# A fifth expert slot, scatter halves around the transposes, streamed shared weights and an earlier router exponential in a hybrid mixture-of-experts trunk

## The chip, the cores and the metric

The kernel runs on one core of a Trainium2 chip. The metric is the device time of one execution in microseconds (us). TensorE (PE) multiplies, VectorE (DVE), ScalarE (ACT) and GpSimd (POOL) do the elementwise work, SyncE (SP) issues the weight transfers, and 16 DMA engines carry them. 1 MiB is 1.049 MB.

## The reference, cut to what matters

Two layers, 256 tokens, width 1024, everything in float32. Each layer is a mixer (layer 0: two sparse-attention groups; layer 1: forgetting attention), a mixture of 64 experts of width 256 with 8 chosen per token plus a shared expert, and a gated per-layer embedding.

```python
for i in range(DEPTH):
    h = even_mixer(...) if i % 2 == 0 else odd_mixer(...)
    x = layer_norm(ALPHA * x + h, ln1_g[i], ln1_b[i])
    m = moe_ffn(x, ...)
    x = layer_norm(ALPHA * x + m, ln2_g[i], ln2_b[i])
    e_i = rms_norm(p[i] @ ple_w_proj[i], ple_norm_g[i])
    x = x + jax.nn.sigmoid(x @ ple_w_gate[i]) * e_i
...
def moe_ffn(x, router_w, router_bias, w1, w3, w2, sw1, sw3, sw2):
    shared = (jax.nn.silu(xf @ sw1) * (xf @ sw3)) @ sw2
    s = jax.nn.sigmoid(xf @ router_w)
    ...                       # 4 of 8 groups, then 8 experts; gates normalised, times 2.5
    # for each expert e, on the tokens that chose it:
    #   y = (silu(xe @ w1[e]) * (xe @ w3[e])) @ w2[e], times its gate, added to its tokens
```

## The kernel before, in words

**Weights.** One expert is w1, w3 and w2 of 1 MiB each (the text calls them gate, lin and down weights), 192 MiB in a layer. All weights of the kernel pass through `ring`, four slots of 3 MiB, in the order of a list `items`: projection pieces, two pieces of the output projection, 64 experts, the embedding's projection and its two gate pieces. SP walks the list and waits before each load for the work that used the slot. In the experts, SP works by pairs (`pair_load`): when PE has done the gate product of pair m (semaphore `exp_gate`), it issues the two gate weights of pair m+2; after the lin product (`exp_up`) the two lin weights; after the down product (`exp_down`) the two down weights. Beside the ring there is spare room (`extra_w1`, `extra_w3`, `extra_w2`, in tiles that are free by then) that takes all of expert 4 and part of expert 10 (`extra_load`, `AGAIN`), and the constants `EARLY` and `NEXT_EARLY` name experts 8 and 14, of which parts go early into the room so won. Expert 4's loads (`extra_load`, L450) are issued when the router's products, the split of x and `y_begin` are done. Experts 0 and 1 are loaded during the attention, 2 and 3 after the output projection.

**The start of a layer's experts.** PE does the output projection, transposes x, and interleaves the router's product with the shared expert's two up products (`shared_up`, L1177: weight columns stationary, 128 tokens moving, 64 products of 128x128 by 128). ACT rounds x to `x_hi` (`x_high`, 2.1 us a tile), copies the transpose, takes the router's exponential and sets `y_acc` to ALPHA * x (`y_begin`); POOL subtracts to get `x_lo`; DVE chooses the experts (`choose`), numbers each expert's tokens (`place`) and builds one-hot matrices.

**The expert loop.** Experts go in 32 pairs; eight experts are an octet of four pairs, u = 0 to 3. Each expert has 64 token slots. `gather` (L1208) fetches an octet's tokens by a product with the one-hot `sel`, a quarter of it in each pair, into one of two sets of buffers (`xe_even`, `xe_odd`). For a pair PE does the gate and the lin product (`exp_up`, L1269, each two experts side by side), the transposes of h (`h_transpose`, L1279), those of the next pair's selection (`sel_transpose`), the down product (`exp_down`, L1309), and the scatter of the pair before (`scatter`, L1331), in two column halves that DVE adds to `y_acc` (`add_y`, L2186). ACT applies SiLU (L1669), which waits for both up products, then copies hT (L1675), and copies y to `y_hi` (L1694); DVE multiplies by the lin half and the slot gate (`gate_h`, L2175), and makes `y_lo` (L2191). One scatter half stands between the gate and the lin product, the other after the transposes, except in the first three and last four pairs, where both stand ahead of the transposes. The shared expert's down products (`shared_down`, L1169) stand in pairs 24 to 27, one each.

**The end.** The last pair's lin and down weights come in column halves. After it: the last scatter, the second norm, the embedding's projection (L1441, waits for its weights) and gate (L1462).

Of the kernel before, what the change touches and what calls it, by code (L numbers as in the profile page):

```python
# [13 lines left out]
P = 128  # L14
# [44 lines left out]
UNROLL = 4  # L59
EARLY = 2 * RING  # L60
AGAIN = EARLY + 2
NEXT_EARLY = AGAIN + RING

# [57 lines left out]
def build_trunk(nc, a, out):  # L121
    with ExitStack() as ctx:
# [5 lines left out]
        def sem(name):  # L128
            if name not in sems:
# [71 lines left out]
        xe_even = (xT[:, :, :].rearrange("p a n -> p (a n)").rearrange("p (c n) -> p c n", c=DC // 2),  # L201
                   proj_flat[:, NT * D:2 * NT * D].rearrange("p (c n) -> p c n", c=DC // 2))
        xe_odd = (pT[:, :, :].rearrange("p a n -> p (a n)").rearrange("p (c n) -> p c n", c=DC // 2),
                  gb_row[:, :, :].rearrange("p a n -> p (a n)").rearrange("p (c n) -> p c n", c=DC // 2))

        def xe(odd, c):

            return (xe_odd if odd else xe_even)[c // 4][:, c % 4, :]

        def xe_two(odd, c):  # L210
            return (xe_odd if odd else xe_even)[c // 4][:, c % 4:c % 4 + 2, :]
# [9 lines left out]
                    (h_silu_all, router_w[:, :, :].rearrange("p c n -> p (c n)")))  # L221
        h_silu = roped[:, 0, 1536:1792]
# [9 lines left out]
        ple_pT = pT[:, 0, 0:512].rearrange("p (c n) -> p c n", c=2)  # L232
# [77 lines left out]
        loaded, w1_loaded_at, down_loaded_at = [], [], []  # L310
        total, w1_total, down_total = [0] * RING, [0] * RING, [0] * RING
        for k, (parts, (_, _, e)) in enumerate(items):
            ffn = parts == "expert"

            signals = not (parts == "expert" and e >= UNROLL and e % 2)
            early = ffn and e == EARLY + 1
            total[k % RING] += 16 * ((1 if ffn else len(parts)) if signals or early or e == NE - 1 else 0)
            down_total[k % RING] += 32 if parts == "expert" and e >= NE - 2 else 16 if ffn and (signals or e == NEXT_EARLY + 1) else 0
            w1_total[k % RING] += 16 if ffn and (signals or early or e == NEXT_EARLY + 1) else 0
            loaded.append(total[k % RING])  # L320
            w1_loaded_at.append(w1_total[k % RING])
            down_loaded_at.append(down_total[k % RING])
# [95 lines left out]
        def _(sp):  # L418
# [1916 lines left out]
```

## Time and profile before

| | |
|---|---|
| median of 3 runs | 1345.64 us (1344.99 to 1346.11) |
| the profiled execution's own time | 1344.79 us |
| its span | 1342.9 us, TensorE clock 1.00 of full speed |
| busy: PE, PE weight loads, DVE, ACT, POOL | 97%, 56%, 35%, 23%, 6% |
| moved by DMA | 462.0 MB, mean 344 GB/s |

The span runs from the first to the last instruction of the profiled execution. Matmuls are pipelined and their ends are modelled, so a busy PE says that PE had work, not that nothing held it back; what it waited for stands in the timeline in brackets, and which stretches were bound by weights shows in the step from pair to pair. Windows give the DMA engines' busy share and their GB/s; those are the rows to read beside PE.

### The profile page before, as it was taken

What the parts mean: (1) busy time and instruction counts of PE and PEld (TensorE: products, weight loads), DVE (VectorE), ACT (ScalarE), POOL (GpSimd) and SP (SyncE); (2) the same over time, 40 slices, a digit from 0 to 9 for tenths busy, and PEclk for the clock granted to TensorE, in tenths of its full rate; (3) what the DMA queues carried; (4) which work ended last, traced back from release to release, by engine and by line L of the source; (5) the groups of instructions that cost most, each with busy time, mean ns of one, the idle gap of its engine ahead of it and who ended that gap; (6) DMA issues with size and microseconds to landing.
All of it is one profiled execution on the core that took longest, in us unless ns stands there. A gap on an engine that the chain in (4) does not pass through costs nothing.

```text
span 1342.9 us, 23014 instructions
## 1 busy us (share of the span) xinstructions
PE 1301.0 (97%) x9694; PEld 746.3 (56%) x9694; DVE 475.1 (35%) x791; ACT 310.3 (23%) x747; POOL 81.2 (6%) x93
## 2 busy tenths in 40 slices
PE   9999999999999999998999999999999999999988
PEld 4555665555555455554488457555555555555544
DVE  1584533333332323333511246232333323233244
ACT  1244422121221221111210234222122221112112
POOL 2443100000000000000100021000000000000000
PEclk9999999999999999999999999999999999999999
DMA  9820689999999999999764537899999999999991
GB/s 306 308 96 32 251 304 415 420 420 421 421 421 420 421 420 420 421 421 394 246 234 145 197 112 277 323 410 421 419 420 421 421 420 421 421 421 421 420 383 76
DMA packets 83151, 462.00 MB, mean 344 GB/s; under 512 B 7024, under 2 KB 7504, under 8 KB 34672
## 3 DMA queue, kind: packets, MB, share of 16 engines
q1 hardware_dynamic: 81040, 454.15, 83.7%
q0 software_dynamic: 2016, 6.43, 1.6%
q8 instruction: 79, 1.29, 0.4%
q14 instruction: 16, 0.13, 0.0%
HBM read 459.50 MB, written 1.05 MB: 343 GB/s over the span
## 4 chain that ended last, share of the span: by engine, by line
PE 78%; DMA 18%; DVE 2%; issue 1%; ACT 0%; SPq 0%; DVEq 0%
PE ps L1269 27%; DMA ring<-in_exp_w_dram 17%; PE ps L1309 12%; PE ps L1331 4%; PE ps L918 4%; PE ps L1462 4%; PE ps L1208 4%; PE ps L1105 3%; PE ps L1023 3%; PE ps L1177 2%; PE ps L1129 2%; PE ps L1279 1%; PE ps L1169 1%; PE ps L1080 1%; PE ps L1441 1%
## 5 line engine op out<-in xcount | busy, mean ns | idle before, releaser
L1309 PE MATMUL ps<-ring,qkT 128*32 128x512 f32 x1984 | 232.9, 595 | 4.1 <-issue 2.8
L2186 DVE TENSOR_TENSOR o_tok<-ps,o_tok 128x1024 f32<-128x1024 f32 x124 | 150.6, 1222 | 156.4 <-PE ps L1331 156.4
L2191 DVE TENSOR_TENSOR y_lo<-ps,y_hi 128x1024 fp32r<-128x1024 f32 x62 | 75.9, 1224 | 213.6 <-ACT y_hi L1694 213.6
L1269 PE MATMUL ps<-ring,xT 128*64 128x256 f32 x1008 | 124.5, 385 | 14.7 <-DMA ring<-in_exp_w_dram 14.6
L1309 PEld LDWEIGHTS ps<-ring,qkT 128*32 128x32 f32 x1984 | 61.5, 109 | 128.8 <-issue 127.6
L1269 PE MATMUL ps<-ring,pT 128*64 128x256 f32 x992 | 124.3, 385 | 5.9 <-DMA ring<-in_exp_w_dram 5.8
L1669 ACT ACTIVATE roped<-ps 128x256 f32<-128x256 f32 x64 | 24.6, 384 | 454.6 <-PE ps L1269 454.6
L1269 PE MATMUL ps<-ring,proj 128*64 128x256 f32 x1008 | 121.8, 379 | 0.0
L1269 PE MATMUL ps<-ring,gb_row 128*64 128x256 f32 x992 | 121.5, 379 | 0.0
L2175 DVE SCALAR_TENSOR_TENSOR roped<-roped,rows,ps 128x256 f32<-128x256 f32 x64 | 30.7, 480 | 236.6 <-ACT roped L1669 236.6
L1269 PEld LDWEIGHTS ps<-ring,xT 128*64 128x64 f32 x1008 | 71.0, 136 | 73.6 <-issue 35.8
L1269 PEld LDWEIGHTS ps<-ring,pT 128*64 128x64 f32 x992 | 69.2, 136 | 67.7 <-issue 36.2
L1694 ACT ACTIVATE y_hi<-ps 128x1024 fp32r<-128x1024 f32 x62 | 63.4, 1023 | 182.9 <-PE ps L1309 182.9
L1269 PEld LDWEIGHTS ps<-ring,proj 128*64 128x64 f32 x1008 | 76.7, 137 | 32.6
L1269 PEld LDWEIGHTS ps<-ring,gb_row 128*64 128x64 f32 x992 | 74.6, 137 | 33.4
L1208 PE MATMUL ps<-sel,x_hi 128*128 128x256 f32 x256 | 69.6, 306 | 0.0
L1208 PE MATMUL ps<-sel,x_lo 128*128 128x256 f32 x256 | 63.3, 281 | 0.0
L1208 PEld LDWEIGHTS ps<-sel,x_hi 128*128 128x128 f32 x256 | 48.3, 189 | 22.4 <-issue 22.4
L1331 PE MATMUL ps<-y_hi,selT 64*128 64x512 f32 x248 | 60.7, 486 | 0.0
L648 POOL DMA_DIRECT2D gb_row<-in_ple_norm_g_dram x2 | 1.5, 737 | 952.0 <-DVEq L1959 952.0
L918 PE MATMUL ps<-ring,xT 128*128 128x512 f32 x128 | 57.8, 600 | 0.0
L1462 PE MATMUL ps<-ring,xT 128*128 128x512 f32 (+1 forms) x144 | 55.9, 546 | 0.7 <-ACT xT L1473 0.7
(308 smaller groups left out, 1464.3 us busy)
## 6 DMA issues: line engine op xcount, KB each, us to landing
ring<-in_exp_w_dram SPq DMA_DIRECT2D x158, 2048.0 KB, 22.8
ring<-in_exp_w_dram SPq DMA_DIRECT2D x54, 1024.0 KB, 8.8
ring<-in_od_w_in_dram SPq DMA_DIRECT2D x6, 2048.0 KB, 8.6
ring<-in_ple_w_gate_dram SPq DMA_DIRECT2D x4, 2048.0 KB, 15.4
ring<-in_ev_w_in_dram SPq DMA_DIRECT2D x3, 2048.0 KB, 20.0
ring<-in_ev_w_o_dram SPq DMA_DIRECT2D x2, 2048.0 KB, 10.4
x_tok<-in_exp_w_dram SPq DMA_DIRECT2D x4, 1024.0 KB, 7.6
ring<-in_exp_w_dram SPq DMA_DIRECT2D x8, 512.0 KB, 17.9
```

Of the source, the lines that this page charges most:

```text
L918: ins = pe.matmul(ps[:, 2 * t + n, :], xT[:, c, t * P:(t + 1) * P], w[:, c, :], start=(c == 0), stop=(c == DC - 1))
L1023: ins = pe.matmul(ps[:, proj_bank(j, t), 0:c1 - c0], xT[:, c, t * P:(t + 1) * P], w[:, c, :], start=(c == 0), stop=(c == DC - 1))
L1105: ins = pe.matmul(ps[:, (2 * j + half) % 4, b * SEQ:(b + 1) * SEQ], w[:, c, (2 * half + b) * P:(2 * half + b + 1) * P], xT[:, c, :], start ...
L1208: ins = pe.matmul(by_tile[:, :, t, :], part[:, t, (2 * j + c) * P:(2 * j + c + 1) * P], sel[:, t, :].rearrange("p (e s) -> p e s", e=8), s ...
L1269: ins = pe.matmul(ps[b * SLOTS:(b + 1) * SLOTS, 2, w * FE:(w + 1) * FE], xe(odd, c)[:, u * P + b * SLOTS:u * P + (b + 1) * SLOTS], views[b ...
L1309: ins = pe.matmul(ps[q:q + TILE_SLOTS, 4 + half, :], hT[:, f, h0:h0 + TILE_SLOTS], down_rows(b, f, half), start=(f == 0), stop=(f == 1))
L1331: ins = pe.matmul(ps[:, bank + t, :], selT[tile_rows(t), par, :], part[tile_rows(t), half * PIECE:(half + 1) * PIECE], start=(part is y_hi ...
L1462: ins = pe.matmul(ps[:, part_bank(t, n, i), cols], xT[:, c, t * P:(t + 1) * P], w[:, c, cols], start=(c == 0), stop=(c == DC - 1), skip_gr ...
L1694: act.activation(y_hi[:, :], ps[:, 4:6, :], ACT.Copy).then_inc(sem("y_high"), 1)
L2175: dve.scalar_tensor_tensor(h_exp, h_silu, slot_gate[:, par:par + 1], ps[:, 2, FE:2 * FE], ALU.mult, ALU.mult)\
L2186: dve.tensor_tensor(ys, ps[:, bank:bank + 2, :], ys, ALU.add).then_inc(sem("y_added"), 1)
L2191: dve.tensor_tensor(y_lo[:, :], ps[:, 4:6, :].rearrange("p b n -> p (b n)"), y_hi[:, :], ALU.subtract)\
```

## The change

- The ring's four slots, the spare room (`FIFTH`) and, for expert 1 alone, one more room (`APART`: `o_tok`, half of `qkT`, `gb_row`) become homes of experts: 0 to 4 by `EARLY_HOMES`, all others by `CYCLE`, five homes in turn. Slot 0, which held expert 1, now takes expert 5 at that place. Everything is loaded in single experts of three loads of 1 MiB; the fifth home's down weights are three loads, row f = 0 in pieces of 4 KB, row f = 1 in two column halves with pieces of 2 KB.
- `pair_load(L, m)` frees by rooms: after pair 0 only expert 6 is loaded, after pair 1 experts 7 and 8, then 2m+5 and 2m+6; after pair 28 experts 61 and 62, after pair 29 expert 63 and the halves.
- Expert 1's gate weights are requested ahead of the shared expert's, expert 4's lin and half of its down weights behind those; the rest of experts 1 and 4 after the split of x (`fifth_load`). `y_begin` moves from ACT to POOL, after the first gate product.
- `shared_up` has the tokens stationary and the weights moving (32 products of 128x128 by 256); the shared h is transposed in pair 24 (`shared_turn`), and its down products go to pairs 25, 26, 28 and 29. The transposes of p move inside pair 28.
- `router_exp` stands ahead of `x_high`; the placing product waits for `chosen` and not for the gates.
- In the loop, gate and lin products stand back to back (banks 2 and 3), SiLU waits for the gate product alone, one scatter half stands ahead of the transposes and one behind; the whole gather of the next octet is in u = 3, with one set of buffers.

```diff
-UNROLL = 4
-EARLY = 2 * RING
-AGAIN = EARLY + 2
-NEXT_EARLY = AGAIN + RING
+FIFTH = RING
+APART = RING + 1
+EARLY_HOMES = (3, APART, 1, 2, FIFTH)
+CYCLE = (0, 3, 1, 2, FIFTH)
+SHARED_TURN = PAIRS - 8
+SHARED_AT = (PAIRS - 7, PAIRS - 6, PAIRS - 4, PAIRS - 3)
+
+
+def home(e):
+
+    return EARLY_HOMES[e] if e < len(EARLY_HOMES) else CYCLE[e % len(CYCLE)]
+
+
+def room_of(e):
+
+    return {6: 0, 7: 2, 8: 3}.get(e, e - len(CYCLE))
...
+            def pair_load(L, m):
+
+                after = [e for e in range(6, NE) if room_of(e) // 2 == m]
+                whole = [e for e in after if e < NE - 2]
+                sp.wait_ge(sem("exp_gate"), L * PAIRS + m + 1)
+                for e in after:
+                    gate_load(L, e)
+                sp.wait_ge(sem("exp_up"), L * PAIRS + m + 1)
+                for e in whole:
+                    lin_load(L, e)
+                if NE - 1 in after:
+                    last_lin_load(L)
+                sp.wait_ge(sem("exp_down"), L * PAIRS + m + 1)
+                for e in whole:
+                    down_load(L, e)
+                if NE - 1 in after:
+                    last_down_load(L)
...
+            def apart_gate_load(L):
+
+                if L == 0:
+                    sp.wait_ge(sem("qkT_tp"), len(QKT_BATCHES) + NT)
+                else:
+                    sp.wait_ge(sem(f"ple_out{L - 1}"), 2 * NT)
+                gate_load(L, 1)
+
+            def fifth_load(L):
 
                 sp.wait_ge(sem("router_mm"), NT * (L + 1))
                 sp.wait_ge(sem("x_split"), NT * (L + 1))
-                sp.wait_ge(sem("y_begun"), NT * (L + 1))
-                sp.dma_start(extra_w1, a["exp_w1"][L, RING].rearrange("(p c) f -> p c f", c=DC)).then_inc(sem("extra_loaded"), 16)
-                sp.dma_start(extra_w3, a["exp_w3"][L, RING].rearrange("(p c) f -> p c f", c=DC)).then_inc(sem("extra_loaded"), 16)
-                extra_down_load(L, RING)
-
-            def extra_down_load(L, e):
-
-                rows_f = a["exp_w2"][L, e].rearrange("(p f) n -> p f n", f=2)
-                for f in range(2):
-                    if f:
-                        sp.wait_ge(sem("shared_h"), NT * (L + 1))
-                    for half in range(2):
-                        sp.dma_start(extra_w2[f][half], rows_f[:, f, half * PIECE:(half + 1) * PIECE]).then_inc(sem("extra_loaded"), 16)
+                gate_load(L, 4)
+                sp.wait_ge(sem("shared_w1_used"), L + 1)
+                lin_load(L, 1)
+                sp.wait_ge(sem("gb_used"), NT * (3 * L + 1))
+                down_load(L, 1)
+                sp.wait_ge(sem("shared_h"), NT * (L + 1))
+                down_load(L, 4, (1,))
...
                     if k == e0 + 2:
+                        apart_gate_load(L)
                         shared_load(L)
+                        lin_load(L, 4)
+                        down_load(L, 4, (0,))
...
+                pool.wait_ge(sem("exp_gate"), L * PAIRS + 1)
+                for t in range(NT):
+                    step(pool.tensor_tensor(y_acc[:, t, :].rearrange("p (n c) -> p n c", c=DC),
+                                            x_hi[:, t, :].rearrange("p (c n) -> p n c", c=DC),
+                                            x_lo[:, t, :].rearrange("p (c n) -> p n c", c=DC), ALU.add))
+                    pool.tensor_scalar(y_acc[:, t, :], y_acc[:, t, :], ALPHA, None, ALU.mult).then_inc(sem("y_begun"), 1)
...
-                def shared_up(t, blocks):
-
-                    for n in blocks:
-                        for c in range(DC):
-                            ins = pe.matmul(ps[:, 4 + t, n * P:(n + 1) * P], (shared_w1, shared_w3)[n // 2][:, c, n % 2::2],
-                                            xT[:, c, t * P:(t + 1) * P], start=(c == 0), stop=(c == DC - 1))
+                def shared_up(t, w, c0, c1):
+
+                    for c in range(c0, c1):
+                        ins = pe.matmul(ps[:, 4 + t, w * FE:(w + 1) * FE], xT[:, c, t * P:(t + 1) * P],
+                                        (shared_w1, shared_w3)[w][:, c, :], start=(c == 0), stop=(c == DC - 1))
                     return ins
 
+                def shared_turn():
+
+                    pe.wait_ge(sem("shared_h"), NT * (L + 1))
+                    pe.wait_ge(sem("y_added"), 2 * (L * PAIRS + SHARED_TURN - 1))
+                    for f in range(2):
+                        for t in range(NT):
+                            ins = pe.transpose(ps[:, 1, f * SEQ + t * P:f * SEQ + (t + 1) * P],
+                                               h_all[:, t * FE + f:(t + 1) * FE:2], ident)
+                    ins.then_inc(sem("shared_tp"), 1)
...
+                def pe_step(m, o, u, gather_next=True, selT_next=True, scatter_last=True):
 
                     par = u % 2
-                    inside = scatter_last and gather_next and not (o == 0 and u < 3)
-                    late = o == 0 and u == 3
-                    exp_up(m, o, odd, u, par, first and M0 == 0, scatter_half=inside, gather_inside=late)
-                    if scatter_last and not inside:
-                        if o == 0:
-                            pe.wait_ge(sem("xe_copied"), 4 * O0 + 5)
+                    gathers = gather_next and u == 3
+                    if m + M0 > 0:
+                        pe.wait_ge(sem("exp_h"), m + M0)
+                    if m > 0:
+                        pe.wait_ge(sem("selT_copied"), m + (M0 + 1))
+                    exp_up(m, o, u, 0)
+                    if gathers:
                         scatter(m - 1, 0, 1 - par)
-                        scatter(m - 1, 1, 1 - par, bank=0)
-                    own_gather = gather_next and (o > 0 or u == 0)
-                    if own_gather or late:
-                        j = 2 if late else u
-                        pe.wait_ge(sem("xe_copied"), 4 * o + (4 * O0 + 4 + j))
-                        if m >= PAIRS - 8:
-                            pe.wait_ge(sem("shared_added"), 4 * L + m - (PAIRS - 8) + 1)
-                        gather(o + 1, j, halves=(0, 1) if scatter_last else (0,))
+                    if m == PAIRS - 4:
+                        pe.wait_ge(sem("xe_copied"), 4 * OCTETS + 4 * O0)
+                        pe.wait_ge(sem("y_added"), 2 * (M0 + m - 1))
+                        for t in range(NT):
+                            for c in range(2):
+                                ins = pe.transpose(ps[:, 0, c * SEQ + t * P:c * SEQ + (t + 1) * P], p_tok[:, t, c::2], ident)
+                            ins.then_inc(sem(f"pT_tp{L}"), 1)
+                    if m == SHARED_TURN:
+                        shared_turn()
+                    if m in SHARED_AT:
+                        shared_down(SHARED_AT.index(m))
+                    if gathers:
+                        gather(o + 1, 0)
+                    exp_up(m, o, u, 1)
+                    if gathers:
+                        scatter(m - 1, 1, 1 - par)
+                    elif scatter_last:
+                        scatter(m - 1, 0, 1 - par)
                     h_transpose(m)
                     if selT_next:
                         sel_transpose(m + 1, o + 1 if u == 3 else o, (u + 1) % 4)
-                    if own_gather and not scatter_last:
-                        gather(o + 1, u, halves=(1,))
-                    if inside:
-                        scatter(m - 1, 1, 1 - par)
-                    exp_down(m, par, first and M0 == 0, by_half=not selT_next)
-                    if late:
-                        pe.wait_ge(sem("xe_copied"), 4 * O0 + 7)
-                        gather(1, 3)
-
+                    if scatter_last and not gathers:
+                        if m == SHARED_TURN:
+                            pe.wait_ge(sem("shared_hT"), L + 1)
+                        if m in SHARED_AT:
+                            pe.wait_ge(sem("shared_added"), 4 * L + SHARED_AT.index(m) + 1)
+                        scatter(m - 1, 1, 1 - par, bank=0)
+                    if gathers:
+                        pe.wait_ge(sem("xe_copied"), 4 * o + (4 * O0 + 5))
+                        gather(o + 1, 1)
+                    exp_down(m, 0, by_half=not selT_next)
+                    if gathers:
+                        pe.wait_ge(sem("xe_copied"), 4 * o + (4 * O0 + 6))
+                        gather(o + 1, 2)
+                    exp_down(m, 1, by_half=not selT_next)
+                    if gathers:
+                        pe.wait_ge(sem("xe_copied"), 4 * o + (4 * O0 + 7))
+                        gather(o + 1, 3)
...
-                def y_begin(t):
-                    act.activation(y_acc[:, t, :], x_tok[:, t, :], ACT.Copy, scale=ALPHA).then_inc(sem("y_begun"), 1)
-
                 rsqrt_guess()
-                x_high(0)
                 copy_T("xT_act", tp, 0)
                 router_exp(0)
-                y_begin(0)
+                x_high(0)
                 rsqrt_guess()
-                x_high(1)
                 copy_T("xT_act", tp, 1)
                 router_exp(1)
-                y_begin(1)
+                x_high(1)
                 shared_silu(0)
                 shared_silu(1)
...
-                    act.wait_ge(sem("exp_up"), m + (M0 + 1))
+                    act.wait_ge(sem("exp_gate"), m + (M0 + 1))
```

## Rows read from the trace of the kernel before

**Rows 1.** The page: GB/s in 40 slices, and the chain's shares.

```profile
GB/s 306 308 96 32 251 304 415 420 420 421 421 421 420 421 420 420 421 421 394 246 234 145 197 112 277 323 410 421 419 420 421 421 420 421 421 421 421 420 383 76
...
PE 78%; DMA 18%; DVE 2%; issue 1%; ACT 0%; SPq 0%; DVEq 0%
```

**Rows 2.** PE's timeline, one pair: start, duration, line; down products at 408.19 and 422.07.

```profile
408.19 3.64 PE L1309 MATMUL ps<-ring,qkT 128*32 128x512 f32 x32
...
419.73 0.38 PE L1208 MATMUL ps<-sel,x_hi 128*128 128x256 f32 x1
...
420.80 0.50 PE L1279 MATMUL ps<-const,roped 128*128 128x128 f32 x2
...
422.07 3.64 PE L1309 MATMUL ps<-ring,qkT 128*32 128x512 f32 x32
```

**Rows 3.** PE's waits between 200 and 700 us: total, times, longest.

```profile
PE ps L1269 <- DMA ring<-in_exp_w_dram: 10.8, 16, 1.7
```

**Rows 4.** PE's timeline, the last two pairs of layer 0.

```profile
612.72 1.95 PE L1269 MATMUL ps<-ring,xT 128*64 128x256 f32 x16 [1.68 <-DMA ring<-in_exp_w_dram]
...
618.47 3.64 PE L1309 MATMUL ps<-ring,qkT 128*32 128x512 f32 x32 [0.34 <-issue]
622.77 1.95 PE L1269 MATMUL ps<-ring,xT 128*64 128x256 f32 x16 [0.66 <-DMA ring<-in_exp_w_dram]
...
631.97 3.64 PE L1309 MATMUL ps<-ring,qkT 128*32 128x512 f32 x32 [0.52 <-issue]
```

**Rows 5.** Windows of layer 0; last two columns: DMA engines' busy share, GB/s.

```profile
180.00:185.00 5.00, 5.00 (x47) 3.25 (x44) 0.00 (x0) 0.28 (x1) 0.00 (x0) 1.00 0.52 184
185.00:190.00 5.00, 4.60 (x42) 2.04 (x45) 0.48 (x1) 1.83 (x6) 0.00 (x0) 1.00 1.00 423
190.00:194.00 4.00, 4.00 (x40) 2.33 (x34) 1.23 (x1) 1.02 (x1) 0.00 (x0) 1.00 0.91 348
...
195.00:200.00 5.00, 4.50 (x45) 2.74 (x45) 1.82 (x3) 1.07 (x5) 0.00 (x0) 1.00 1.00 356
...
280.00:400.00 120.00, 120.00 (x1041) 64.17 (x1038) 39.38 (x45) 27.21 (x63) 0.00 (x0) 1.00 1.01 420
```

**Rows 6.** The same windows view, two stretches with pieces of 2 KB.

```profile
14.00:22.00 8.00, 8.00 (x20) 3.61 (x19) 0.13 (x1) 0.60 (x1) 2.40 (x5) 1.00 1.05 388
...
224.00:228.00 4.00, 4.00 (x37) 2.55 (x37) 0.48 (x1) 1.45 (x3) 0.00 (x0) 1.00 1.02 364
```

**Rows 7.** The chain before the experts of layer 0 (first and last part of four).

```profile
155.43 5.65 PE ps L1177 x48
...
171.67 1.94 PE ps L1177 x16
```

**Rows 8.** One line, L1105 (layer 1's projection): duration min/median/max, first and last start.

```profile
L1105 PE MATMUL ps<-xT,ring x192: 379/379/380, 693.6 to 734.8; 128*128 128x256 f32 x192
```

**Rows 9.** SP's timeline: the first loads after pairs 0 and 1.

```profile
181.26 0.33 SPq L495 DMA_DIRECT2D ring<-in_exp_w_dram  x1
...
194.30 0.38 SPq L530 DMA_DIRECT2D ring<-in_exp_w_dram  x1
```

**Rows 10.** DMA issues: KB each, median us from issue to landing.

```profile
qkT<-in_sh_w_dram SPq DMA_DIRECT2D x2, 1024.0 KB, 4.7
```

**Rows 11.** PE's timeline, pairs 0 and 1 of layer 0.

```profile
184.60 0.39 PE L1208 MATMUL ps<-sel,x_hi 128*128 128x256 f32 x1
...
185.74 0.50 PE L1279 MATMUL ps<-const,roped 128*128 128x128 f32 x2 [0.40 <-DVE roped L2175]
...
199.95 0.64 PE L1309 MATMUL ps<-ring,qkT 128*32 128x512 f32 x4 [0.50 <-ACT qkT L1675]
```

**Rows 12.** The chain of waits at the end of layer 1's experts.

```profile
1301.66 0.78 issue
```

**Rows 13.** ACT's and POOL's timelines: router exponential, then x_lo of tile 1.

```profile
165.60 0.22 ACT L1629 ACTIVATE rows<-ps 128x64 f32<-128x64 f32 x1 [1.01 <-PE ps L883]
...
162.89 2.87 POOL L705 TENSOR_TENSOR x_lo<-x_tok,x_hi 128x1024 fp32r<-128x1024 f32 x1 [13.79 <-ACT x_hi L1624]
```

More of the change, by code:

```diff
@@ L306, in release_value @@
             return sem(f"ple_mm{L}"), NT * 2 + n if n else NT
[L310 to L322, printed above, removed]
-        w_loaded = [sem(f"w_loaded{s}") for s in range(RING)]
-        down_loaded = [sem(f"down_loaded{s}") for s in range(RING)]
-        w1_loaded = [sem(f"w1_loaded{s}") for s in range(RING)]
+        assert all(expert_item[L] % RING == EARLY_HOMES[0] for L in range(DEPTH))
+        loaded, gate_at, lin_at, down_at = {}, {}, {}, {}
+        gate_total, lin_total, down_total = [0] * (APART + 1), [0] * (APART + 1), [0] * (APART + 1)
+        for k, (parts, (_, L, e)) in enumerate(items):
+            if parts != "expert":
+                lin_total[k % RING] += 16 * len(parts)
+                loaded[k] = lin_total[k % RING]
+                continue
+            at = home(e)
+            gate_total[at] += 16
+            lin_total[at] += 16
+            down_total[at] += 48 if at == FIFTH else 32 if e >= NE - 2 else 16
+            gate_at[L, e], lin_at[L, e], down_at[L, e] = gate_total[at], lin_total[at], down_total[at]
+        w_loaded = [sem(f"w_loaded{s}") for s in range(APART + 1)]
+        down_loaded = [sem(f"down_loaded{s}") for s in range(APART + 1)]
+        w1_loaded = [sem(f"w1_loaded{s}") for s in range(APART + 1)]
         def slot_view(k, n, c):
@@ new lines, in ffn_load, with last_lin_load @@
+            def ffn_load(L, e):
+                gate_load(L, e)
+                lin_load(L, e)
+                down_load(L, e)
+            def last_lin_load(L):
+                s, e = home(NE - 2), NE - 2
+                for half in range(2):
+                    cols = slice(half * UP_N // 2, (half + 1) * UP_N // 2)
+                    sp.dma_start(ring[:, s:s + 2, UP_N + cols.start:UP_N + cols.stop],
+                                 a["exp_w3"][L, e:e + 2].rearrange("e (p c) f -> p e (c f)", c=DC)[:, :, cols])\
+                      .then_inc(w_loaded[s + half], 16)
@@ L565, in _ @@
+                    if k == e0 + RING:
+                        fifth_load(L)
+                        for m in range(PAIRS - 2):
+                            pair_load(L, m)
                         k = e0 + NE
@@ L1677, in selT_copy @@
                 def selT_copy(m, par):
-                    bank = 3 if isinstance(m, int) and m == 0 else 2
+                    bank = 6 if isinstance(m, int) and m == 0 else 2
                     act.wait_ge(sem("selT_tp"), m + (M0 + 1))
@@ L2237, in dve_step @@
                         y_low(m)
-                    if build_bf and u == 2:
+                    if gather_next and u == 2:
                         sel_bf_build(o + 1)
```

421 lines of the change are left out of this document (171 added, 250 removed).

## The prediction

> **What bounds the kernel now.** I read the page first, then windows, PE's timeline, PE's waits, SP's timeline and the chain. The page's slices show two long plateaus at 420 GB/s, one for each layer's experts, and idle DMA engines between them [rows 1]. The chain gives PE 78% and DMA 18% [rows 1], which alone would call it a PE kernel. The step from pair to pair says more. Undisturbed, one pair takes PE 13.9 us (408.19 to 422.07) [rows 2]. Its weights, 6 MiB or 6.29 MB at 420 GB/s [rows 5], take 15.0 us, or 2.5 us for 1 MiB. So PE eats up what was loaded ahead and then waits: 16 times in layer 0, 10.8 us in all [rows 3], the last times at 612.72 and 622.77 [rows 4]. From 185 us on the DMA engines never rest (busy share 0.91 to 1.01 [rows 5]). A layer's end is thus set by three things: how many weights are there when the unbroken stream begins, how fast the stream runs, and how much PE work remains after the last arrival that PE waits for. PE's own order inside a pair counts only where PE isn't waiting for weights, so SiLU's earlier start, the scatter halves and the gathers gathered into u = 3 gain nothing in mid-loop as long as they add less than the 10.8 us of waits. A pair without a gather falls by the 1.1 us of one (419.73 to 420.80 [rows 2]), one with u = 3 rises by three times that, and five homes hold 15 MiB, 37 us of stream, which bridges the uneven pairs. I cost all of it at nothing; with that cover gone it would be 0.1 to 0.2 us a pair.
>
> **Part by part, layer 0; layer 1 repeats it.**
>
> (a) *The lead of the stream.* Before, experts 0 to 4 (15 MiB) are in by 180 us, and the next requests go out at 181.26, when pair 0's gate product is done [rows 9]. Afterwards expert 5 takes the place of 1, and 1 and 4 use the idle time, so 18 MiB are in; but pair 0 frees room for expert 6 alone, and 7 and 8 must wait for pair 1's gate product. When is that? The shared products shrink from 128 entries at 5.65/48 = 0.118 us [rows 7], 15.1 us, to 64 entries at 41.2/191 = 0.216 us [rows 8], 13.8 us: the loop starts 1.3 us earlier. Pair 0 loses a gather of 1.1 us that covered waits, and gets the waits instead: gate_h alone, some 0.7 of the 1.14 us between 184.60 and 185.74, and the 0.5 us for hT that pair 1 shows at 199.95 [rows 11]; the balance is 0.3 us less. So the request seen at 194.30 [rows 9] goes out at 192.7, and with a start-up of 4.7 - 2.5 = 2.2 us [rows 10] the stream is unbroken from 194.9 with 21 MiB in. Before, by then: 15 MiB and (184 + 423) x 5 + 348 x 4.9 = 4.7 MB [rows 5], 19.5 MiB, and then 195 to 200 runs at 356 instead of 420 GB/s, 0.3 MiB lost. The lead is 1.8 MiB: **-4.5 us** (-3 if the new stream has the same slow stretch and a later start, -5.5 at most).
>
> (b) *Small pieces.* Eleven experts in the stream (9, 14, ... 59) now bring their down weights half in pieces of 4 KB, half in 2 KB. The long stretch of 2 KB pieces ran at 388 GB/s [rows 6]: half a MiB costs 0.10 us more than at 420, the 4 KB half I put at half that, 0.15 x 11 - 0.2 for expert 10, which had such pieces before: 1.4 us. The stretch that holds expert 10's pieces ran at 364 GB/s for 4 us [rows 6]: what it carried would take 3.5 us at 420, 0.5 us for 1 MiB, so 0.25 + 0.13 in eleven experts, less 0.5: 3.7 us. I take **+2.2 us**, nearer the first, which is the longer sample. The Trainium skill (DMA: Bandwidth & Descriptors, Specifications) puts the smallest transfer at line rate at 512 B; by it these pieces cost nothing and the sum would be 2.2 us a layer lower. Both windows here speak against it.
>
> (c) *The order of the last loads.* Before, the gate weights of pair 31 come 4 MiB behind the lin weights of pair 30: 10.05 us (612.72 to 622.77 [rows 4]) and PE, which needs 10.05 - 0.66 - 0.34 = 9.05 us for the work between, has to wait for them. Afterwards pair 30 is experts 60 and 61 from different requests: lin 61 is followed by down 61, gate 63 and then the last halves. PE waits for lin 61 and then still has 9.05 us of work, while gate 63 lands after 5.0 us. So pair 31 begins 4.05 us behind the stream, where before it began with it: **+4.0 us** (0 if PE were not held at lin 61 at all, 4.5 if pairs 28 and 29, which now carry shared products behind the heavy pair 27, leave it later still).
>
> (d) *The last pair.* A scatter half between transposes and down product covers the 0.52 us wait at 631.97 [rows 4]: **-0.5 us**. The Exp ahead of the rounding, and the placing product without the gates, lie beside shared products that keep PE busy: nothing.
>
> (e) *After layer 1* PE stands 0.78 us before the embedding's projection, whose weights are behind the stream [rows 12]; a lead of 2 us removes it: **-0.7 us**, once. y_begin on POOL: two adds of 2.87 us [rows 13] and two scalings lie between pair 0's gate product and the first add_y some 18 us later: nothing.
>
> Sum: 2 x (-4.5 + 2.2 + 4.0 - 0.5) - 0.7 = +1.7 us, so 1346.5 us against the profiled execution's 1344.79 (span 1342.9 and 1.9 around it). The median of the runs is 0.85 us above that execution: **1347.3 us**, 0.1% more. What a measurement of this kernel tells from no change is about 0.2%, 2.7 us, so this is no change.
>
> **Rivals.** *The tail costs nothing* (c = 0): PE reaches pair 30 late anyway, or lin 61 arrives early because the DMA engines finish unevenly, and the lead reaches the end: 1347.3 - 8.0 = 1339.3. For it: the stretches of waiting are short; against: 1.68 us of waiting at just that place [rows 4]. *Small pieces cost nothing*: the DMA engines move pieces of 2 and 4 KB at the rate of 8 KB, and 1347.3 - 2 x 2.2 = 1342.9 remains; both windows [rows 6] are against it. (This is how the Trainium skill's page named in (b) has it.) *Small pieces are dear*, 3.7 us a layer as in the shorter window: 1347.3 + 2 x 1.5 = 1350.3. *Expert 1 comes late*: its lin weights are asked for only after the split of x, behind expert 4's gate weights. The exponential at 165.60 moves up about a microsecond, then rounding (2.1) and x_lo of 2.87 us [rows 13] end the split at about 170, where it ended at 165.8; plus 2.2 and two MiB, it lands at 177.2. PE wants it 3.55 us into the loop, at 179.8. It decides from 2.6 us of delay, and then every microsecond is paid in both layers, for the stream waits on PE there. With 3 us: 1353.3. For it: SP's queue holds expert 1's down weights, expert 4's rest and all of pair_load behind that one wait.
>
> **How the numbers follow.** Likeliest, the sum as it stands: 0.42, own range 1344 to 1349. Tail free 0.17, pieces free 0.11: together 0.28 faster by over 0.2%. Pieces dear 0.14, expert 1 late 0.16: 0.30 slower. Within 0.2%: 0.42. The range 1338.5 to 1352 leaves out the outer part of the late expert (0.1) and the two gains together (0.05).
>
> **What would show it.** Right: windows at 420 GB/s from about 195 us; steps of some 12.7 and 17 us early in the loop; PE's first waits for weights near pair 14, earlier than pair 18, because it runs faster; a wait before pair 30's lin product and none before pair 31's gate product; L1177 at 13.8 us a layer. Wrong: a wait at pair 31 too (then c is too high), windows clearly below 415 GB/s in the loop (b too low), a wait in pair 0 for weights (the late expert), or waits for ACT or DVE in most pairs, which would make PE's own order the bound.

## The result, and the profile after

The changed kernel is slower by a little: 1350.76 us against 1345.57 us (medians of 6 runs each), a ratio of 1.0038, 95% interval 1.0026 to 1.005, so 5.2 us. A second measurement of both gave 1349.55 against 1344.37 us, 1.0037 (1.0022 to 1.0053). The profiled execution took 1350.55 us, with a span of 1348.4 us, 5.5 us more than before.

The page of the changed kernel: GB/s in 40 slices and the chain's shares.

```profile
GB/s 306 306 95 63 297 272 418 418 419 418 421 418 419 419 420 418 419 419 370 230 220 159 197 126 269 323 420 418 419 419 419 418 420 420 419 418 419 419 355 63
...
PE 77%; DMA 11%; DVE 6%; SPq 4%; issue 1%; ACT 1%; DVEq 0%
```

Beside [rows 1] three things stand out. The plateaus lie for the most part at 418 to 419 GB/s where they lay at 420 to 421. The DMA share of the chain fell from 18% to 11%, but SP's queue (SPq) rose from 0% to 4%: the chain now runs in part through SP's issue of loads, some of which held SP for 2.13 us and more. PE itself waits for weights nearly as long as before, 9.8 us in layer 0 for 10.8. And VectorE (DVE), at 2% before, now has 6% of the chain. That last figure points to the part of the change that I had costed at nothing; the chain has 19.2 us of VectorE between 150 and 185 us, and 5.4 us in the kernel of experiment one.

**Where the time went.** I took three distances in PE's timeline, for each layer, in every kernel: from the first shared product (L1178, before L1177) to the first gate product of the expert loop; from the down product of pair 0 to that of pair 31; and the sum that a layer's stretch makes, first shared product to pair 31's down product.

```
us, layer 0 / layer 1         shared to loop   pair 0 to pair 31   whole stretch
before                        22.29 / 22.29    444.95 / 444.18     476.71 / 475.94
changed                       23.82 / 23.85    445.89 / 445.90     478.67 / 478.80
changed, second profile       23.85 / 23.84    445.49 / 445.76     478.29 / 478.65
```

The stretch grew by 2.0 and 2.9 us. The forecast was +1.2 in each layer. After layer 1 the 0.78 us of [rows 12] are gone (pair 31's down product to the embedding's projection: 5.42 us, before 6.25). In this one execution PE's granted clock also fell to half in layer 1's attention, and the stretch from layer 0's last down product to layer 1's first shared product took 189.86 us for 188.28. So 1.96 + 2.86 - 0.83 + 1.58 = 5.6 us, less 0.1 us at the start of the program: the 5.5 us of the span.

**The prologue.** PE's timeline of the changed kernel from the first shared product to the first gather, layer 0 (start, duration, line; idle before in brackets). Neighbours in this pipelined view overlap, so read the starts.

```profile
155.17 3.62 PE L1178 MATMUL ps<-qkT,xT 128*128 128x256 f32 x16
158.62 2.32 PE L1178 MATMUL ps<-pT,xT 128*128 128x256 f32 x10
161.71 1.16 PE L721 MATMUL ps<-const,x_tok 128*128 128x128 f32 x8 [0.76 <-DVEq L1951]
...
169.24 1.89 PE L1178 MATMUL ps<-pT,xT 128*128 128x256 f32 x8
172.20 0.66 PE L1204 MATMUL ps<-roped,const 128*128 128x64 f32 x4 [1.08 <-DVE roped L1928]
172.70 1.95 PE L1178 MATMUL ps<-pT,xT 128*128 128x256 f32 x8
174.81 0.36 PE L1220 MATMUL ps<-sel,x_hi 128*128 128x256 f32 x1 [0.17 <-DVE sel L2138]
```

The shared products are as cheap as I said: 16 of them from 155.17 to 158.62, 0.216 us each, 13.8 us for 64. But PE stands idle three times, 2.0 us in all, each time for VectorE, and none of these waits was there before. What holds VectorE shows in its own timeline and in GpSimd's (POOL), here in layer 1, tile 0:

```profile
820.57 0.15 DVE L1919 MATCH_REPLACE8 rows<-rows 128x8 f32<-128x8 f32 x1
820.75 2.22 DVE L1921 TENSOR_SCALAR rows<-rows 128x8 f32<-128x8 f32 x1
823.01 0.23 DVE L1924 SCALAR_TENSOR_TENSOR rows<-rows 128x64 f32<-128x64 f32 x1
...
820.09 2.86 POOL L699 TENSOR_TENSOR x_lo<-x_tok,x_hi 128x1024 fp32r<-128x1024 f32 x1 [29.88 <-ACT x_hi L1624]
```

A tensor_scalar of 8 elements a partition takes 2.22 us. It ends at 822.97, and GpSimd's subtraction, under way since 820.09, ends at 822.95. The source view has all four of them, one a tile:

```profile
L1921 DVE TENSOR_SCALAR rows<-rows x4: 2207/2274/2328, 152.2 to 837.3; 128x8 f32<-128x8 f32 x4
```

The same instruction before, L1929, took 171 to 172 ns in all four places. There the rounding on ScalarE came first and x_lo ran while VectorE stood waiting for the router's exponential. In layer 1, tile 1, the kernel before shows (VectorE, then GpSimd):

```profile
830.85 0.20 DVE L1917 TENSOR_SCALAR rows<-rows 128x64 f32<-128x64 f32 x1 [3.18 <-ACT rows L1629]
...
827.86 2.88 POOL L705 TENSOR_TENSOR x_lo<-x_tok,x_hi 128x1024 fp32r<-128x1024 f32 x1 [13.77 <-ACT x_hi L1624]
```

x_lo sat in a gap of 3.18 us and was over 0.1 us before VectorE went on. The change put it behind the exponential and the 2 us of the rounding, and so into the router's chain. (The Trainium skill, "SBUF — State Buffer", Who interferes with whom, has this as an exclusive lock: VectorE and GpSimd share one pair of ports, a tensor_scalar can use it, and whoever comes second is blocked until the other's instruction ends. The rows agree, 822.97 beside 822.95.)

**The tail.** PE's waits for weights from 200 to 700 us, where [rows 3] had 16 of 10.8 us:

```profile
PE ps L1264 <- DMA ring<-in_exp_w_dram: 8.2, 9, 1.3
PE ps L1264 <- DMA x_tok<-in_exp_w_dram: 1.6, 1, 1.6
```

The last of them is at 504.38 us. From there to the end of the layer PE never waits for weights, where it waited at 612.72 and 622.77 before [rows 4]. Layer 1 is the same but for one wait of 0.44 us at 1238.92, and the second profile has two such short ones (0.17 and 0.37 us). Eight steps of PE alone (pair 23's down product at 515.86 to pair 31's at 633.84, 118.0 us) set the end.

**The stream.** Windows of the changed kernel, answering to [rows 5], and SP's first requests, answering to [rows 9]:

```profile
180.00:185.00 5.00, 5.00 (x50) 3.34 (x48) 0.00 (x0) 0.64 (x4) 0.00 (x0) 1.00 0.55 185
185.00:190.00 5.00, 3.85 (x39) 1.69 (x39) 1.15 (x3) 0.70 (x4) 2.85 (x1) 1.00 0.91 339
190.00:195.00 5.00, 5.00 (x48) 2.68 (x42) 1.23 (x1) 1.02 (x1) 4.91 (x3) 1.00 0.51 162
195.00:200.00 5.00, 5.00 (x47) 3.00 (x43) 0.48 (x1) 0.56 (x2) 4.91 (x2) 1.00 0.89 341
280.00:400.00 120.00, 119.64 (x1027) 64.57 (x1024) 37.44 (x42) 29.99 (x64) 0.00 (x0) 1.00 1.02 419
```

```profile
182.71 0.33 SPq L437 DMA_DIRECT2D ring<-in_exp_w_dram  x1
...
195.23 1.05 SPq L437 DMA_DIRECT2D ring<-in_exp_w_dram  x2
```

The requests behind pair 1's gate product go out at 195.23 instead of the 192.7 I forecast. By 200 us the changed kernel has moved 44.1 MB, the kernel before 43.0 MB (windows of 0 to 200 us): a lead of 1.1 MiB, not 1.8. At 419 GB/s against 421 a part of it is lost on the way.

### The profile page after: what moved, and what is told of

Read it like the earlier page. It is cut to its first block, busy times and chain, and to the rows that moved or that the text cites. A ratio compares the mean times of both kernels' runs of the same rounds, so it can differ in the third digit from the quotient of the medians.

```text
span 1348.4 us, 22909 instructions
## 1 busy us (share of the span) xinstructions
PE 1306.5 (97%) x9574; PEld 739.7 (55%) x9574; DVE 485.1 (36%) x793; ACT 317.4 (24%) x743; POOL 108.0 (8%) x101
## 4 chain that ended last, share of the span: by engine, by line
PE 77%; DMA 11%; DVE 6%; SPq 4%; issue 1%; ACT 1%; DVEq 0%
PE ps L1264 26%; PE ps L1294 13%; DMA ring<-in_exp_w_dram 7%; PE ps L1220 5%; PE ps L1317 4%; PE ps L1462 4%; DMA x_tok<-in_exp_w_dram 4%; PE ps L919 3%; PE ps L1106 3%; PE ps L1024 3%; PE ps L1130 2%; PE ps L1274 2%; SPq L462 1%; SPq L437 1%; PE ps L1081 1%
## 5 line engine op out<-in xcount | busy, mean ns | idle before, releaser
L1264 PE MATMUL ps<-ring,xT 128*64 128x256 f32 x1632 | 247.2, 384 | 11.7 <-DMA ring<-in_exp_w_dram 8.8
L1264 PE MATMUL ps<-ring,pT 128*64 128x256 f32 x1632 | 242.7, 379 | 0.0
L1264 PEld LDWEIGHTS ps<-ring,xT 128*64 128x64 f32 x1632 | 138.1, 137 | 101.9 <-issue 51.7
L1264 PEld LDWEIGHTS ps<-ring,pT 128*64 128x64 f32 x1632 | 146.7, 137 | 57.2
L1294 PEld LDWEIGHTS ps<-ring,qkT 128*32 128x32 f32 x1632 | 56.8, 109 | 106.0 <-issue 103.3
L1668 ACT ACTIVATE qkT<-ps 128x256 f32<-128x256 f32 x64 | 24.6, 385 | 240.3 <-PE ps L1274 239.2
L1294 PE MATMUL ps<-roped,qkT 128*32 128x512 f32 x288 | 67.6, 597 | 0.0
L1656 ACT ACTIVATE xT<-ps 128x1024 f32<-128x1024 f32 x32 | 32.7, 1025 | 86.5 <-PE ps L1264 71.4
L1264 PE MATMUL ps<-proj,xT 128*64 128x256 f32 x192 | 45.9, 382 | 4.9 <-DMA ring<-in_exp_w_dram 4.9
## 6 DMA issues: line engine op xcount, KB each, us to landing
ring<-in_ple_w_gate_dram SPq DMA_DIRECT2D x4, 2048.0 KB, 12.6
roped<-in_exp_w_dram SPq DMA_DIRECT2D x24, 256.0 KB, 19.2
```

The costliest lines, as they stand in the source:

```text
L1264: ins = pe.matmul(ps[b * SLOTS:(b + 1) * SLOTS, 2 + w, w * FE:(w + 1) * FE], xe(c)[:, u * P + b * SLOTS:u * P + (b + 1) * SLOTS], views[b] ...
L1294: ins = pe.matmul(ps[q:q + TILE_SLOTS, 4 + half, :], hT[:, f, h0:h0 + TILE_SLOTS], down_rows[b](f, half), start=(f == 0), stop=(f == 1))
L1656: act.activation(xe_two(2 * j), ps[:, bank:bank + 2, :], ACT.Copy).then_inc(sem("xe_copied"), 1)
```

## The experiments

Each ran beside the kernel before on the same chip. Ratios are to it, with the 95% interval; the changed kernel stands at 1.0037 or 1.0038 by the same measure.

**One: the rounding ahead of the exponential again.**

```diff
 rsqrt_guess()
+x_high(0)
 copy_T("xT_act", tp, 0)
 router_exp(0)
-x_high(0)
 rsqrt_guess()
+x_high(1)
 copy_T("xT_act", tp, 1)
 router_exp(1)
-x_high(1)
```

> The changed kernel with ScalarE's rounding of x put back ahead of the router's exponential. Theory H (GpSimd's subtraction x_lo now lies over the router's chain on VectorE and holds its tensor_scalar L1921 for 2.2 us instead of 0.17, once for each tile): L1921 falls to 0.17 us, PE's waits of 0.76 us before the transposes of tile 1 and of 1.08 us before the placing product go, the expert loop starts about 2.8 us earlier in each layer, and 4 to 5.5 us come off in all: 1345 to 1347 us. Rival (VectorE's chain is late because the shared product takes PE less time, whatever the order on ScalarE): L1921 may fall, but the loop starts where it did, 1350 to 1351 us. Rival (the tail decides, PE has no room from 504 us on, and what the prologue gains is waited for at the weights): the loop starts earlier, and the time falls by under 1.5 us.

Measured: 1344.66 us, 0.9998 (0.9989 to 1.0007), by the ratios 0.4% or 5.4 us less than the changed kernel. The source view:

```profile
L1921 DVE TENSOR_SCALAR rows<-rows x4: 171/172/172, 152.8 to 832.8; 128x8 f32<-128x8 f32 x4
```

The waits before the transposes and the placing product are gone, and the shared products reach the loop in 21.41 and 21.43 us, 2.4 us sooner than in the changed kernel and 0.9 sooner than before. Theory H holds, and the rival of the tail falls: the layer ends sooner by the same 2.4 to 2.8 us. The start moved a little less than the 2.8 us that I expected.

**Two: the exponential ahead of the rounding, in the kernel before.** The mirror image of the same lines in the kernel before, with y_begin still behind each.

> The kernel before with the exponential put ahead of the rounding, that part of the change alone. Theory H: the tensor_scalar L1929 takes 2.2 us instead of 0.17 for each tile; about 1 us of the first hold is covered by VectorE's wait for the products (0.98 us), the second is not, so the placing product waits 2 to 3 us and the loop starts 2 to 3 us later a layer: 1348.5 to 1351.5 us. Rival (the exponential comes earlier, the chain is shorter or the same): 1344.5 to 1346 us.

Measured: 1353.73 us, 1.0064 (1.0049 to 1.0078). The hold appears in the kernel that had none:

```profile
L1929 DVE TENSOR_SCALAR rows<-rows x4: 2212/2299/2381, 154.3 to 838.9; 128x8 f32<-128x8 f32 x4
```

PE waits 0.75 us before the transposes and 1.65 us before the placing product, and the loop starts 2.9 us later in layer 0. The sign and the place are as H says; the time is above what I expected. In the profiled execution 2.0 us of the rest lie before the experts of layer 0, and 1.5 us are a fall of PE's clock behind the wait of 1.66 us in layer 1 (granted 0.52 from 844 to 846 us). Why the median of the runs is as high, I haven't settled.

**Three: the shared products earlier.**

```diff
-SHARED_TURN = PAIRS - 8
-SHARED_AT = (PAIRS - 7, PAIRS - 6, PAIRS - 4, PAIRS - 3)
+SHARED_TURN = 16
+SHARED_AT = (17, 18, 20, 21)
```

(VectorE's loop over the octets ends at octet 3, so that pairs 16 to 23 stand with fixed numbers.)

> The changed kernel with the shared expert's transposes in pair 16 and its four down products in pairs 17, 18, 20 and 21, where PE waits for weights, instead of pair 24 and pairs 25, 26, 28 and 29. Theory T (from 504 us on PE never waits for weights again, so the 9.5 us of shared work in the last eight pairs are on the path): waits for weights appear again before the last pairs, and a layer ends 1.5 to 3 us sooner, 1345 to 1348 us. Rival (the stream sets the end and the shared work is hidden in it wherever it stands): 1350 to 1351.5 us. Rival (shared work in pairs 17 to 21 delays the down products and with them the requests): slower than 1351.5 us.

Measured: 1347.46 us, 1.0019 (1.001 to 1.0028), by the ratios 2.5 us less than the changed kernel. The waits are back, 7.8 us of them from 510 us on in layer 0, the last two before pair 30's down product:

```profile
611.41 1.95 PE L1264 MATMUL ps<-ring,xT 128*64 128x256 f32 x16 [0.88 <-DMA ring<-in_exp_w_dram]
616.38 1.95 PE L1264 MATMUL ps<-ring,xT 128*64 128x256 f32 x16 [1.29 <-DMA ring<-in_exp_w_dram]
...
621.96 3.64 PE L1294 MATMUL ps<-ring,qkT 128*32 128x512 f32 x32
634.39 1.92 PE L1294 MATMUL ps<-ring,qkT 128*32 128x512 f32 x16
```

But the stretch is shorter by only 0.4 and 0.8 us (478.25 and 478.02 against 478.67 and 478.80; against the second profile of the changed kernel, 478.29 and 478.65, by 0.04 and 0.6). Experiment six repeats the 0.4 and 0.8 against one. So the shared work did set the end, and the stream stood about a microsecond or less behind it. My 1.5 to 3 us a layer were too high, by the medians (1.2 a layer) too, though the time lies in the range that I gave. Part of the medians' 2.5 us stands in none of the three distances.

**Four: the fifth home's down weights whole.** From expert 9 on they go to gb_row, which expert 1 has left, in pieces of 8 KB.

```diff
-down_total[at] += 48 if at == FIFTH else ...
+down_total[at] += 48 if e == FIFTH else ...
...
-elif to == APART:
+elif to == APART or e > FIFTH:
     sp.dma_start(first_w2[:, :, :], rows_f).then_inc(down_loaded[to], 16)
```

> The changed kernel with the down weights of experts 9, 14, ..., 59 loaded as one piece of 8 KB a partition into gb_row, which expert 1 has left, instead of one piece of 4 KB and two of 2 KB. Theory P (the small pieces slow the stream, term b): the windows of the loop rise from 418 to 419 to 420 to 421 GB/s, PE's last wait for weights in the layer comes about 1.3 us sooner, and so does the layer's end: 1347.5 to 1349.5 us. Rival (small pieces cost nothing, the slower stream has another cause): windows at 418 to 419 and 1350 to 1351.5 us. Rival (they cost what b's upper bound said, 0.34 us an expert): 1344 to 1346 us.

Measured: 1346.35 us, 1.0004 (0.9993 to 1.0016). The window of 280 to 400 us:

```profile
280.00:400.00 120.00, 120.00 (x1032) 64.51 (x1027) 37.43 (x42) 30.22 (x64) 0.00 (x0) 1.00 1.01 421
```

421 for 419 GB/s, and pair 0 to pair 31 takes 444.31 and 444.39 us for 445.89 and 445.90: 1.5 us a layer (1.2 and 1.4 against the second profile, 445.49 and 445.76). That is theory P by the windows and the distances. The time is lower than I expected for it (1347.5 to 1349.5): the median fell by 4.4 us, 3.1 of them in these stretches, the rest in none of the three distances. The DMA engines are busy all through both windows (1.02 and 1.01), so it is the rate of the pieces and no pause of the stream; and SP's queue, 4% of the chain in the changed kernel, is at 0% here.

**Five: x_lo in four instructions of a quarter each**, in the order of the changed kernel.

> The changed kernel with GpSimd's x_lo of each tile made in four instructions of a quarter each (about 0.72 us) instead of one of 2.86 us; order and results as before. Theory H as a lock held for one instruction: L1921 waits for the end of the quarter under way at most, 0.3 to 0.9 us instead of 2.2, the loop starts 1 to 2.4 us earlier a layer, 1345.5 to 1349 us. Rival (VectorE and GpSimd share bandwidth for as long as GpSimd is at work): L1921 stays at 2.2 us, 1350 to 1351.5 us. Rival (GpSimd's queue takes the lock again before VectorE gets it): L1921 at 1.5 to 2.2 us, no gain.

Measured: 1347.1 us, 1.0009 (1.0 to 1.0017). VectorE in layer 1, tile 1, while GpSimd's quarters (0.86 us each) run from 834.13 to 837.43:

```profile
834.69 0.33 DVE L1924 TENSOR_SCALAR rows<-rows 128x8 f32<-128x8 f32 x1
835.05 0.83 DVE L1927 SCALAR_TENSOR_TENSOR rows<-rows 128x64 f32<-128x64 f32 x1
835.92 0.23 DVE L1928 MAX8 rows<-rows 128x8 f32<-128x64 f32 x1
...
836.73 0.78 DVE L1933 TENSOR_TENSOR gates<-rows,roped 128x64 f32<-128x64 f32 x1
```

The tensor_scalar takes 0.22 to 0.33 us instead of 2.2 (L1924 is L1921 with three lines more above it), though GpSimd is at work just as long. So the hold lasts as long as one instruction of the other engine and no more, and shared bandwidth is ruled out. The loop starts after 22.14 us instead of 23.85. Two more instructions are held here: the scalar_tensor_tensor and the tensor_tensor, both with both tensors in SBUF and 0.22 us elsewhere, take 0.83 and 0.78. Each held instruction ends 0.02 to 0.08 us after a GpSimd quarter, as the whole holds of 2.2 us end 0.02 to 0.03 us after the whole subtraction. MAX8 beside the same quarters isn't held (0.23 us, as in the kernel before).

**Six to eight: the edits together.** Six is one and three, seven is one, three and four, and eight is seven with this:

```diff
 for e in after:
-    gate_load(L, e)
+    if e != NE - 2:
+        gate_load(L, e)
 sp.wait_ge(sem("exp_up"), L * PAIRS + m + 1)
 for e in whole:
     lin_load(L, e)
+if NE - 2 in after:
+    gate_load(L, NE - 2)
```

> Both: the rounding ahead of the exponential, and the shared products in pairs 16 to 21. In the two single runs the layer from pair 0's to pair 31's down product took 445.5 and 445.9 us with the first, 445.5 and 445.1 us with the second, against 445.9 in the changed kernel, so the stream stands right behind PE in the tail. If the two add up, the loop starts 2.4 us earlier as in the first and the tail is 0.4 to 0.8 us a layer shorter as in the second: 1342.5 to 1344 us. If the first's lead of the stream comes free only with a light tail, 1340 to 1342 us.

> The same two and the down weights of experts 9, 14, ..., 59 in pieces of 8 KB. Alone, this took 1.5 us a layer off the loop (444.3 and 444.4 instead of 445.9 us). With a tail that is bound by the stream, the whole difference of 418.7 to 421 GB/s over 440 us counts, 2.4 us a layer: 1338 to 1340.5 us. Rival (the shared products of the tail were what the stream hid, and nothing adds up): 1341 to 1344 us.

> The kernel with all three, and expert 62's gate weights asked for behind expert 61's lin weights instead of ahead of them. Step c of the prediction (PE is held at lin 61 and pair 31 then begins behind the stream): lin 61 lands 2.5 us earlier, PE's waits before pair 30's down product, 2.2 us in the run with the early shared products, go or fall below 0.7 us, and 1.5 to 2.2 us a layer come off against the kernel with all three. Rival (the last pair's weights bind as soon as lin 61 does not): the waits move to pair 31 and under 0.7 us a layer is gained.

```
                        median   ratio, 95% interval        shared to loop   whole stretch, layer 0 / 1
one                     1344.66  0.9998 (0.9989 to 1.0007)  21.41            475.86 / 476.37
six (one, three)        1342.71  0.9984 (0.9975 to 0.9993)  21.42            475.51 / 475.60
seven (and four)        1339.42  0.9958 (0.9945 to 0.9971)  21.41            473.85 / 474.09
eight (and gate 62)     1336.14  0.9937 (0.9924 to 0.995)   21.41            473.16 / 472.64
```

The edits add up. Six is 0.4 and 0.8 us a layer below one, as three was below the changed kernel. Seven takes 1.7 and 1.5 us more off, less than the 2.4 that I expected for a tail bound by the stream, and eight 0.7 and 1.5 us in the profiled executions, 3.3 us in the medians; in layer 0 that is less than the 1.5 to 2.2 us that I expected, and its profiled execution had a fall of the clock there (561.8 us). Seven's tail, PE's timeline:

```profile
606.40 1.95 PE L1266 MATMUL ps<-ring,xT 128*64 128x256 f32 x16 [0.73 <-DMA ring<-in_exp_w_dram]
611.37 1.95 PE L1266 MATMUL ps<-ring,xT 128*64 128x256 f32 x16 [1.30 <-DMA ring<-in_exp_w_dram]
616.96 3.64 PE L1296 MATMUL ps<-ring,qkT 128*32 128x512 f32 x32
629.39 3.64 PE L1296 MATMUL ps<-ring,qkT 128*32 128x512 f32 x32
```

PE is held at pair 30's gate and lin products (2.03 us) and at nothing behind them. In eight, layer 0, both waits are gone, and the two down products stand at 615.08 and 627.52; in layer 1 one of 0.73 us is left. Eight is the fastest of all: 0.6% below the kernel before, 1.0% below the changed one.

**Nine and ten: the order of the last loads alone, and the changed kernel again.**

> The changed kernel with nothing but expert 62's gate weights asked for behind expert 61's lin weights. Theory T (in the changed kernel PE has 118 us of work behind its last wait for weights in layer 0, so the order of the last loads cannot show): the down product of pair 31 follows that of pair 23 at the same distance as before the edit, 118 us, and the time is that of the changed kernel within 0.7 us. Rival (the order of the last loads costs its 1.9 us a layer here too, as it did in the kernel with all three edits): 3 to 4 us less.

> The changed kernel, unedited, beside the run before on the same chip. Every theory: 1349.5 to 1351.5 us, L1921 at 2.2 us. Whether the TensorE clock falls to half in layer 1's attention again (it did in the profiled execution at 771 us, for 3.3 us) is open: if it is part of the change, it should be there again; if it is a matter of the single execution, it may stand elsewhere or be missing, and the span is then some 1.6 us shorter.

Measured: 1349.53 us, 1.004 (1.0028 to 1.0053), and 1349.55 us, 1.0037 (1.0022 to 1.0053). The edit that is worth 3.3 us behind the other three is worth nothing alone: pair 23's to pair 31's down product takes 118.33 us with it and 118.23 without. The second profile of the changed kernel shows no fall of the clock (span 1346.5 us), so that fall is no part of the change.

## Why the prediction was right or wrong

The forecast was 1347.3 us, 0.1% more; it came to 1350.76, inside the range, but 0.38% more: one of the "slower" outcomes that had 0.30, not "no change". The sum had a term missing and a mechanism in the wrong place. That it came so near is luck in part, for the two errors have opposite signs. With the missing term taken out (experiment one), the stretches are 0.8 us shorter and 0.4 us longer than before, where the sum has +1.2 in each layer: what it does contain is 2.0 and 0.8 us too high, and what it lacks is 2.8 and 2.4 us. The time lands on the 1350.3 of *small pieces are dear*, but not for that reason.

**The step that failed** is the sentence in (d) that "the Exp ahead of the rounding" lies "beside shared products that keep PE busy: nothing". It costs 2.4 us at the start of each layer's loop, by experiment one, and it is the whole loss: without it the kernel measures the same as before. I had the rows in hand, x_lo of 2.87 us and the exponential [rows 13], and moved x_lo only as far as the split of x was concerned, not against the instructions that it would now lie beside on another engine. Nor had the exponential anything to gain: PE's router products of tile 1 ended at 830.56 us in the kernel before, and the exponential began at 830.59. The rounding ahead of it had never delayed it. Moved ahead, it began at 165.93 us in layer 0, where [rows 13] had 165.60; the prediction had it about a microsecond sooner.

**(a), the lead.** The shared products shrank by the 1.3 us forecast, and the hold ate that and 1.5 us more, so the loop began later instead of earlier, and the lead was 1.1 MiB for 1.8. With the hold removed (experiment one) it is 1.8 MiB at 200 us, as worked out: 193 GB/s over 140 us and 298 over 60, 44.9 MB, against 43.0. The 4.5 us of it reach the end only in part. Eight, with (b), the tail's shared work and the order of the last loads mended, is 3.6 and 3.3 us a layer below the kernel before, where (a) and (d) promised 5.0.

**(b), small pieces.** Right in mechanism; for +2.2 us a layer the distances show 1.2 to 1.7 (experiments four and seven), the medians 2.2 and 1.6. The rival *small pieces cost nothing*, which is how the Trainium skill would have it (DMA: Bandwidth & Descriptors, Specifications), falls by experiments four and seven. So does *small pieces are dear*.

**(c), the last loads.** Right as a mechanism and wrong for this kernel. It assumed that PE is held at lin 61. In the changed kernel PE isn't held at pairs 28 to 31 in either layer, because pair 24 to pair 29 carry the shared work and pair 27 a whole gather; experiment nine shows the order to cost nothing there. My own bracket, "4.5 if pairs 28 and 29 leave it later still", named the ground and not the consequence: if PE is late by itself, the loads' order doesn't enter at all. In its place stands PE's own work, only 0.4 to 0.8 us a layer ahead of the stream (experiment three). Once PE is held at lin 61, in seven, waits stand where (c) put them and none before pair 31, and a single MiB moved back is worth 1.6 us a layer by the medians, 0.7 and 1.5 by the distances; (c)'s full 4.0 was not tested.

**(d) and (e).** The last pair's wait of 0.52 us is gone, and so are the 0.78 us behind layer 1. Both as forecast.

**y_begin on POOL** cost PE nothing, but its margin was less than I said: GpSimd needed 13.6 and 13.4 us for it, with additions of 3.7 to 4.1 us instead of 2.87, and VectorE stood 2.18 us before its first addition in layer 1, which began 0.1 us after GpSimd was done.

**The rivals.** *Expert 1 comes late*, the one that ended slower: the split of x did end later than I put it, at 171.05 us instead of 170, and expert 1's lin weights were requested at 171.51, but PE never waited for them. The kernel is slower, and not for that reason. *The tail costs nothing* had its premise right, PE reaches pair 30 late anyway, and its time wrong, because what makes PE late costs as well.

**Signs.** Right: L1178 at 0.216 us a product, 13.8 us for 64, the steps early in the loop in sum (two of 12.6 and two of 15.0 us, rather than three of 12.7 and one of 17), PE's first wait for weights at pair 15, none before pair 31's gate product, windows at 418 to 419, above the 415 that would have spoken against (b). Wrong: the wait before pair 30's lin product, and the start of the unbroken stream. I had listed waits for VectorE only "in most pairs"; the ones that decided were before the loop.

## What to carry to other kernels

Before a step is moved on one engine, look at what it releases on another, and lay that instruction over the third engine's timeline: a long GpSimd instruction in VectorE's idle gap is free, and the same instruction 2 us later held an 8-element operation for 2.2 us on the critical chain. Check first whether the step moved ahead was ever waiting for the one it overtakes. And where PE is loaded at the end of a stretch that the DMA engines bound in the middle, move that work into the middle, where it covers waits; only then does the order of the last loads count.

## What the runs showed of the hardware that was not expected

The hold of VectorE by GpSimd lasts for one GpSimd instruction: 2.2 us beside one of 2.86 us, at most 0.33 us beside four of 0.86 us. Splitting cost GpSimd 0.4 us a tile (3.28 for 2.86) and gave back 1.7 us of the 2.4.

PE's granted clock fell to half for 3.4 us in five of the twelve profiled executions, each time within 1.1 us behind an idle stretch of PE. In the changed kernel's profile, windows of 1 us in layer 1's attention, behind two waits of 0.83 and 0.89 us:

```profile
770.00:771.00 1.00, 0.43 (x8) 0.42 (x8) 0.59 (x2) 1.00 (x7) 0.38 (x2) 1.00 1.02 426
771.00:772.00 1.00, 1.00 (x12) 0.64 (x9) 0.00 (x0) 0.95 (x6) 0.85 (x1) 0.51 0.94 385
772.00:773.00 1.00, 1.00 (x6) 0.72 (x4) 0.69 (x1) 0.00 (x0) 0.00 (x0) 0.50 1.08 451
773.00:774.00 1.00, 1.00 (x5) 0.66 (x6) 0.77 (x2) 0.97 (x6) 0.00 (x0) 0.50 1.00 410
774.00:775.00 1.00, 1.00 (x11) 0.59 (x7) 0.00 (x0) 0.54 (x4) 0.99 (x1) 0.78 0.99 418
```

The third column from the end is the clock: 0.50 is 1.2 GHz of 2.4. The same two waits stand in the kernel before and in the second profile of the changed kernel without a fall behind them. It fell behind waits for weights of 2.13 us in experiment four (444 us), 2.31 us in six (1228 us) and 2.13 us in eight (562 us), and of 1.66 us for VectorE in experiment two; a wait of 2.39 us in experiment three had no fall behind it. The stretch of attention around the one shown took 1.6 us longer. In the middle of the expert loop it cost at most little: six's layer with the fall took 475.60 us and the one without 475.51, eight's 473.16 and 472.64. So a wait can cost more than its length, in some executions; what decides it is left open.
